# Closing units in dead activations 4 to 7, earlier opening splits, and the norm's offset added to turned rows

## The reference, cut to what matters

```python
m = hybrid_mixer(x, w_in[l], w_out[l], ...)   # projections, three kinds of attention, output projection
x = layer_norm(ALPHA * x + m, ln1_g[l], ln1_b[l])
hdn = jnp.square(jax.nn.relu(x @ w_up[l]))
x = layer_norm(ALPHA * x + hdn @ w_down[l], ln2_g[l], ln2_b[l])
# layer_norm: (x - mean) * rsqrt(var + eps) * g + b
```

## Time and profile before

| what | us |
|---|---|
| median of 3 runs | 2462.69 (2461.88 to 2463.31) |
| the profiled execution | 2461.92 |
| its span on the core | 2460.2 |
| PE busy | 2431.0 (99% of the span) |
| DVE busy | 1492.9 (61%) |
| ACT busy | 1114.3 (45%) |
| POOL busy | 85.7 (3%) |

### The profile page before, as it was taken

One profiled execution on the slowest core, in us unless ns is written; L12 is line 12 of the kernel. 1 busy time (PEld: TensorE's weight loads), 2 busy tenths in 40 slices (PEclk: granted clock), 3 DMA queues, 4 the chain that ended last, 5 costly groups with the idle time before them and its releaser, 6 DMA issues.

```text
span 2460.2 us, 30027 instructions
## 1 busy us (share of the span) xinstructions
PE 2431.0 (99%) x12624; PEld 2068.1 (84%) x12624; DVE 1492.9 (61%) x1966; ACT 1114.3 (45%) x1489; POOL 85.7 (3%) x94
## 2 busy tenths in 40 slices
PE   9999999999999999999999999999999999999997
PEld 8888888878888888888878888888788888888886
DVE  5576666676556556556665765665765555655566
ACT  4445444444345344344444444543453443443443
POOL 3000000030000000000110000000300000000001
PEclk9999999999999999999999999999999999999999
DMA  8545555655665555555555545556455555556553
GB/s 303 171 158 181 169 168 170 234 173 187 210 197 190 191 188 190 196 191 186 180 166 175 175 161 169 169 170 239 171 189 191 185 199 194 188 189 190 192 196 106
DMA packets 229590, 457.94 MB, mean 186 GB/s; under 512 B 7344, under 2 KB 12208, under 8 KB 228304
## 3 DMA queue, kind: packets, MB, share of 16 engines
q1 hardware_dynamic: 227840, 444.89, 54.5%
q0 software_dynamic: 1616, 11.14, 1.2%
HBM read 452.33 MB, written 3.67 MB: 185 GB/s over the span
## 4 chain that ended last, share of the span: by engine, by line
PE 94%; DVE 4%; ACT 1%; issue 0%; DMA 0%; SPq 0%; ACTq 0%; DVEq 0%
PE pw L469 33%; PE pw L473 16%; PE pw L488 14%; PE pw L490 14%; PE pw L489 14%; DVE w_lo L981 1%; PE pa L545 1%; DVE y L1073 1%; PE pa L621 1%; ACT y L857 1%; PE pa L542 1%; DVE act_a L1042 0%; DMA y<-in_x_dram 0%; ACT w_hi L749 0%; PE pa L629 0%
## 5 line engine op out<-in xcount | busy, mean ns | idle before, releaser
L981 DVE TENSOR_TENSOR w_lo<-raw,w_hi 128x1024 fp32r<-128x1024 f32 (+1 forms) x820 | 985.7, 1217 | 685.2 <-ACT w_hi L749 677.1
L749 ACT ACTIVATE w_hi<-raw 128x1024 fp32r<-128x1024 f32 (+1 forms) x820 | 848.1, 1046 | 1000.3 <-PE pw L490 526.2
L469 PE MATMUL pw<-act_a,w_hi 128*128 128x512 f32 x3456 | 1089.3, 396 | 0.0
L473 PEld LDWEIGHTS pw<-act_a,w_lo 128*128 128x128 f32 x3456 | 649.2, 188 | 153.2
L473 PE MATMUL pw<-act_a,w_lo 128*128 128x256 f32 x3456 | 679.2, 278 | 0.0
L469 PEld LDWEIGHTS pw<-act_a,w_hi 128*128 128x128 f32 x3456 | 528.1, 189 | 1.7
L488 PE MATMUL pw<-w_hi,act_b 128*128 128x512 f32 x1216 | 474.3, 390 | 0.1
L490 PE MATMUL pw<-w_hi,act_b 128*128 128x512 f32 x1216 | 473.2, 389 | 0.0
L489 PE MATMUL pw<-w_lo,act_b 128*128 128x512 f32 x1216 | 473.2, 389 | 0.0
L490 PEld LDWEIGHTS pw<-w_hi,act_b 128*128 128x128 f32 x1216 | 228.2, 188 | 47.8
L488 PEld LDWEIGHTS pw<-w_hi,act_b 128*128 128x128 f32 x1216 | 228.2, 188 | 47.2 <-DVE act_b L1231 0.9
(11 more groups left out here) (151 smaller groups left out, 1100.4 us busy)
## 6 DMA issues: line engine op xcount, KB each, us to landing
raw<-in_w_in_dram SPq DMA_DIRECT2D x128, 1024.0 KB, 5.0
raw<-in_w_up_dram SPq DMA_DIRECT2D x128, 1024.0 KB, 5.3
raw<-in_w_down_dram SPq DMA_DIRECT2D x128, 1024.0 KB, 5.1
raw<-in_w_out_dram SPq DMA_DIRECT2D x32, 1024.0 KB, 5.1
work<-in_ln_g_dram POOLq DMA_DIRECT2D x4, 1024.0 KB, 5.0
work<-in_ln_b_dram POOLq DMA_DIRECT2D x4, 1024.0 KB, 7.4
raw<-in_w_in_dram SPq DMA_DIRECT2D x8, 288.0 KB, 2.9
y<-in_x_dram SPq DMA_DIRECT2D x4, 512.0 KB, 11.0
```

The lines of the kernel that those rows point to most:

```text
L469: nc.tensor.matmul(pw[:, b, :], hi[:, i, cols], act_a[:, k].rearrange("p a t -> p (a t)"), start=(k == 0), stop=False)
L473: last = nc.tensor.matmul(pw[:, b, SEQ:2 * SEQ], lo[:, i, cols], act_a[:, k, 0, :], start=False, stop=(k == KT - 1))
L749: nc.scalar.activation(unit_hi(c, u), raw[:, PAIR * u:PAIR * (u + 1), 0:WIDTH[c]], ACT.Copy) \
L981: V.tensor_tensor(unit_lo(c, u), raw[:, PAIR * u:PAIR * (u + 1), 0:WIDTH[c]], unit_hi(c, u).bitcast(F32), ALU.subtract).then_inc(lo_ready, 1)
```

## The change

It has five parts.

- **Closing units.** Units 4 to 7 of a closing chunk, instead of 0 to 3, lie in the dead activations `act_a`; units 0 to 3 lie in the ring, and are split when the chunk before frees it.
- **Opening splits.** ACT's high splits of opening units 0 to 3 and DVE's low splits 0 to 2 move from `open_block` to the end of `close_block`, among `centre` and `gain`. Opening unit 4 + i waits for closing unit 2i + 1 instead of 7. In `open_block` all four groups of tile 1 are taken, instead of two here and two in the next chunk.
- **The offset.** b of the first three norms is loaded by SP as rows (`b_rows`), turned once (`turn_offsets`) and kept as 48 columns (`b_col`). The turned group no longer has b: `turn_x` waits for `gained`, and `take_x` and `take_x_lo` add a column of b as they read PSUM, in four instructions of 128 columns each instead of one of 512.
- **The residual.** POOL's additions of b to `y` leave the norm: `residual(n)` waits for the last group of tile 1 (`a_ready`), and then for each token tile adds b over all 2048 columns and scales. The last norm keeps `add_offset`. `lambda_sums` of layer 1 waits for the scaling.
- **The turned hidden rows.** PE's two `turn_hidden` move from the opening chunk's unit 5 and the next chunk's unit 1 to units 4 and 5 of the next chunk; the high and low takes of them to its units 6 and 7; `take_hidden_rows` of tile 0 from behind split 2 to behind split 1.

```diff
@@ -286,30 +291,29 @@
-    if CLOSING[c] and u < RING:
-        return act_a[:, LOAD * u:LOAD * u + PAIR].rearrange("p k a t -> p k (a t)")
+    if CLOSING[c] and u >= RING:
+        return act_a[:, LOAD * (u - RING):LOAD * (u - RING) + PAIR].rearrange("p k a t -> p k (a t)")
     if OPENING[c] and u >= RING:
 def unit_lo(c, u):
-    if CLOSING[c] and u < RING:
-        return act_a[:, LOAD * u + PAIR:LOAD * (u + 1)].rearrange("p k a t -> p k (a t)")
+    if CLOSING[c] and u >= RING:
+        return act_a[:, LOAD * (u - RING) + PAIR:LOAD * (u - RING + 1)].rearrange("p k a t -> p k (a t)")
     if OPENING[c] and u >= RING:
-    if CLOSING[c]:
-        if u < RING:
-            return (c - N_OUT if c % NC == LAST_OUT else c - N_OUT, UNITS - 1)
-        return c - 1, u
+    if CLOSING[c] and u >= RING:
+        return c - N_OUT, UNITS - 1
     if OPENING[c] and u >= RING:
-        return c - 1, UNITS - 1
+        return c - 1, PAIR * (u - RING) + 1
     if u >= RING:
         return c, u - RING
-    return c - 1, u if c > 0 and OPENING[c - 1] else u + RING
+    return c - 1, u if OPENING[c] or c > 0 and OPENING[c - 1] else u + RING
...
@@ -326,6 +330,14 @@
+    def load_offsets():
+        for layer in range(DEPTH):
+            for i, src in enumerate((ln1_b, ln2_b)):
+                n = 2 * layer + i
+                if n < 2 * DEPTH - 1:
+                    nc.sync.dma_start(b_rows[n * KT:(n + 1) * KT, :],
+                                      src[layer:layer + 1, :].rearrange("l (k p) -> (l k) p", p=P)).then_inc(b_landed, 16)
...
@@ -414,9 +427,18 @@
-        pool.wait_ge(xt_ps, x_count(e, t, LOADS - 1))
         nc.gpsimd.tensor_scalar(y[:, t, :], y[:, t, :], ALPHA, 1.0, ALU.mult, ALU.mult).then_inc(y_scaled, 1)
+    def residual(n):
+        e = n + 1
+        pool.wait_ge(ln_landed, 32 * (n + 1))
+        pool.wait_ge(a_ready, x_count(e, TT - 1, LOADS - 1))
+        for t in range(TT):
+            nc.gpsimd.tensor_tensor(y[:, t, :], y[:, t, :], ln_b, ALU.add).then_inc(offset_done, 1)
+            pool.wait_ge(offset_done, TT * n + t + 1)
+            scale_y(e, t)
+        pool.wait_ge(y_scaled, TT * (e + 1))
...
@@ -425,26 +447,21 @@
     for t in range(TT):
+        pool.wait_ge(xt_ps, x_count(0, t, LOADS - 1))
         scale_y(0, t)
         load_ln(layer, ln1_g, ln1_b)
-        pool.wait_ge(ln_landed, 64 * layer + 32)
-        for t in range(TT):
-            for j in range(LOADS):
-                add_offset(2 * layer, t, j, x_ready)
-            scale_y(2 * layer + 1, t)
-        pool.wait_ge(x_ready, norm_count(2 * layer, TT - 1, LOADS - 1))
+        residual(2 * layer)
         load_ln(layer, ln2_g, ln2_b)
-        pool.wait_ge(ln_landed, 64 * layer + 64)
-        for t in range(TT):
-            for j in range(LOADS):
-                if layer + 1 < DEPTH:
-                    add_offset(2 * layer + 1, t, j, x_ready)
-                elif t == 0 or j % 2 == 0:
-                    add_offset(2 * layer + 1, t, j, out_ready[t][j])
-            if layer + 1 < DEPTH:
-                scale_y(2 * layer + 2, t)
+        if layer + 1 < DEPTH:
+            residual(2 * layer + 1)
+    n = 2 * DEPTH - 1
+    pool.wait_ge(ln_landed, 32 * (n + 1))
+    for t in range(TT):
+        for j in range(LOADS):
+            if t == 0 or j % 2 == 0:
+                add_offset(n, t, j, out_ready[t][j])
...
@@ -509,7 +526,7 @@
         else:
-            pe.wait_ge(x_ready, norm_count(e - 1, t, j))
+            pe.wait_ge(gained, norm_count(e - 1, t, j))
             if t > 0:
...
@@ -529,6 +546,11 @@
+    def turn_offsets():
+        pe.wait_ge(b_landed, 16 * (2 * DEPTH - 1))
+        n = (2 * DEPTH - 1) * KT
+        nc.tensor.transpose(pa[:, 3, SEQ:SEQ + n], b_rows[:], ident[0:n, 0:n]).then_inc(b_turned, 1)
...
@@ -710,8 +732,8 @@
                         feature_unit(c, u)
-                        if (quarter, j, u) == (0, 1, 1):
-                            turn_hidden(layer, 1)
+                        if (quarter, j) == (0, 1) and 4 <= u < 4 + TT:
+                            turn_hidden(layer, u - 4)
                         continue
...
@@ -770,9 +792,16 @@
         act.wait_ge(xt_ps, x_count(e, t, j))
-        slot = (TT * j + t) % HC if e == 0 else j
-        nc.scalar.activation(act_a[:, HC * j:HC * (j + 1), 0, t * P:(t + 1) * P],
-                             pa[:, slot, :].rearrange("p (i t) -> p i t", i=HC), ACT.Copy).then_inc(a_hi, 1)
+        if e == 0:
+            slot = (TT * j + t) % HC
+            last = nc.scalar.activation(act_a[:, HC * j:HC * (j + 1), 0, t * P:(t + 1) * P],
+                                        pa[:, slot, :].rearrange("p (i t) -> p i t", i=HC), ACT.Copy)
+        else:
+            for i in range(HC):
+                k = HC * j + i
+                last = nc.scalar.activation(act_a[:, k, 0, t * P:(t + 1) * P], pa[:, j, i * P:(i + 1) * P], ACT.Identity,
+                                            bias=b_col[:, (e - 1) * KT + k:(e - 1) * KT + k + 1])
+        last.then_inc(a_hi, 1)
...
@@ -862,27 +891,32 @@
         for j in range(LOADS):
+            if n < 2 * DEPTH - 1 and j % 2 == 0:
+                split_hi(c + 1, j // 2)
             centre(n, 0, j)
+        if n < 2 * DEPTH - 1:
+            split_hi(c + 1, 2)
+            split_hi(c + 1, 3)
         e = n + 1
-        split_hi(c, 0)
+        if n == 0:
+            act.wait_ge(b_col_ready, 1)
         take_x(e, 0, 0)
-        split_hi(c, 1)
-        split_hi(c, 2)
+        split_hi(c, 4)
         take_x(e, 0, 1)
-        split_hi(c, 3)
+        norm_seed(n, 1)
         take_x(e, 0, 2)
-        split_hi(c, 4)
+        split_hi(c, 5)
         take_x(e, 0, 3)
-        split_hi(c, 5)
-        norm_seed(n, 1)
+        centre(n, 1, 0)
         split_hi(c, 6)
-        centre(n, 1, 0)
+        centre(n, 1, 1)
+        centre(n, 1, 2)
         split_hi(c, 7)
-        for j in range(1, LOADS):
-            centre(n, 1, j)
-        for j in range(2):
+        centre(n, 1, 3)
+        for j in range(LOADS):
             take_x(e, 1, j)
...
@@ -908,6 +940,10 @@
                     act.wait_ge(kidx_ps, layer + 1)
+                    if layer == 0:
+                        act.wait_ge(b_turned, 1)
+                        nc.scalar.activation(b_col[:], pa[:, 3, SEQ:SEQ + (2 * DEPTH - 1) * KT], ACT.Copy) \
+                            .then_inc(b_col_ready, 1)
                     nc.scalar.activation(k_idx_t[:], pa[:, 3, 0:SEQ], ACT.Copy).then_inc(kidx_sb, 1)
...
@@ -949,12 +985,8 @@
                 split_hi(c, u)
-                if j == 1 and u < 2:
-                    take_x(2 * layer + 1, 1, 2 + u)
-                if (j, u) == (1, 3):
-                    turned_hidden_hi(layer, 0)
-                if (j, u) == (1, 5):
-                    turned_hidden_hi(layer, 1)
+                if j == 1 and u >= UNITS - TT:
+                    turned_hidden_hi(layer, u - (UNITS - TT))
                 if u == AHEAD - 1 and KIND[c - 1] == "feature":
...
@@ -1038,11 +1070,19 @@
         dve.wait_ge(a_hi, x_count(e, t, j))
-        slot = (TT * j + t) % HC if e == 0 else j
-        V.tensor_tensor(act_a[:, HC * j:HC * (j + 1), 1, t * P:(t + 1) * P],
-                        pa[:, slot, :].rearrange("p (i t) -> p i t", i=HC),
-                        act_a[:, HC * j:HC * (j + 1), 0, t * P:(t + 1) * P].bitcast(F32), ALU.subtract) \
-            .then_inc(a_ready, 1)
+        if e == 0:
+            slot = (TT * j + t) % HC
+            last = V.tensor_tensor(act_a[:, HC * j:HC * (j + 1), 1, t * P:(t + 1) * P],
+                                   pa[:, slot, :].rearrange("p (i t) -> p i t", i=HC),
+                                   act_a[:, HC * j:HC * (j + 1), 0, t * P:(t + 1) * P].bitcast(F32), ALU.subtract)
+        else:
+            for i in range(HC):
+                k = HC * j + i
+                last = V.scalar_tensor_tensor(out=act_a[:, k, 1, t * P:(t + 1) * P], in0=pa[:, j, i * P:(i + 1) * P],
+                                              scalar=b_col[:, (e - 1) * KT + k:(e - 1) * KT + k + 1],
+                                              in1=act_a[:, k, 0, t * P:(t + 1) * P].bitcast(F32),
+                                              op0=ALU.add, op1=ALU.subtract)
+        last.then_inc(a_ready, 1)
...
@@ -1080,6 +1120,9 @@
         dve.wait_ge(lam_landed, 16 * (layer + 1))
+        if layer > 0:
+            dve.wait_ge(y_scaled, TT * (2 * layer + 1))
         did(V.tensor_tensor(lam_products, lam_pairs[:, :, 0, :], lam_pairs[:, :, 1, :], ALU.mult))
...
@@ -1277,29 +1320,32 @@
         for j in range(LOADS):
+            if n < 2 * DEPTH - 1 and j < 3:
+                split_lo(c + 1, j)
             gain(n, 0, j)
         e = n + 1
-        split_lo(c, 0)
+        if n == 0:
+            dve.wait_ge(b_col_ready, 1)
         take_x_lo(e, 0, 0)
-        split_lo(c, 1)
-        split_lo(c, 2)
+        split_lo(c, 3)
         take_x_lo(e, 0, 1)
         aggregate(1)
-        split_lo(c, 3)
+        split_lo(c, 4)
```

(39 more changed lines are left out.)

## The result

The changed kernel takes 2486.94 us (median of 5 runs, 2486.58 to 2489.05), the kernel before 2462.69: 24.3 us more, a ratio of 1.0102 with an interval of 1.0091 to 1.0113. The forecast was 2482, a range of 2463 to 2490, and slower with a chance of 0.77. The profiled execution took 2486.95 with a span of 2485.1, so the spans differ by 24.9.

What follows compares the result with a forecast made beforehand. PE, busy 2431.0 of 2460.2 us, was taken as the bound, with only holes and tail to win. Terms 4.2 - 6.3 - 1.6 + 18.6 + 4.1 + 0.2 = +19.2 us gave 2482 us, range 2463 to 2490.

Steps and rivals of the forecast that it cites:

- The closing chunk: Four closings: DVE's additions with statistics delay unit 4, a hole of 0.9 us, with restart 1.05; +4.2 us in all.
- S+6.35: S is the closing chunk's start; unit 4 was to be ready 6.35 us later, where PE needs it at 5.44.
- The opening chunk: Three openings: earlier splits and no POOL work there start token tile 1 sooner despite finer 128-column instructions; -6.3 us.
- The walk: Step-by-step timing of DVE's opening-chunk instructions, with PE meeting waits of 0.6, 0.5, 1.4 and 0.8 us.
- T+28.15: T is token tile 1's start in the closing chunk; the opening's tile 1 was to start 28.15 us later, against 30.24 before.
- Hidden rows: Moving the turned hidden rows to the next chunk's units 4 and 5 removes a 0.8 us wait, twice; -1.6 us.
- POOL's offset: Behind the first and third boundary, 2048-column additions hold DVE 4.6 us each, so a hidden-rows bank frees late; +18.6 us.
- The rivals that let DVE in or hid POOL's work: DVE gets in during or ahead of POOL's long instruction: some 2466 us, chance 0.16; POOL's work hidden: 2459, 0.10.
- The 144-column chunk: At the second boundary low splits take turns with POOL, delaying unit 3 by 3.1 and unit 4 by 1.0 us; +4.1.
- PE stands for 9.3 us in total in unit 0, twice: PE's wait for hidden-rows banks in the next chunk's first unit, at the first and third boundary; +18.6 us.
- the bank's own term: PE's waits for the hidden-rows banks at the first and third boundary, forecast at +18.6 us.

Runs made afterwards that it cites:

- the closing part alone: The kernel before with only the closing units changed, 4 to 7 in the dead activations and 0 to 3 in the ring: 2466.17 us, ratio 1.0017.
- The run in pieces: The changed kernel with POOL's offset additions in pieces of 512 columns at the same place, scaling still 2048 wide: 2464.73 us, ratio 1.0010.
- the late start: The changed kernel with POOL's residual work after the hidden rows are taken (norms 0, 2) or the 144-column chunk is split (norm 1): 2462.02 us.
- the rows taken one split earlier: The changed kernel with DVE taking the hidden rows of token tile 1 behind low split 2 instead of 3: 2476.36 us, ratio 1.0057.
- the filled stands: The changed kernel with products nobody reads ahead of PE's long waits behind the norms, 30 or 9 of them: 2478.01 us.

## Why the prediction was right, and where it was short

- **The closing chunk.** The step was DVE's two additions in front of low split 4. Unit 4 was to be ready at S+6.35 and PE to lose 1.05; it lost 1.02 in each of four closings, and the closing part alone, on the kernel before, cost 4.07 us for 4.2.
- **The opening chunk.** The walk put token tile 1 at T+28.15, and it came at T+27.8. All four holes are where they were placed, at group 2 (0.4), split 5 (0.5), split 6 (1.3) and tile 1's first group (0.8). The finer instructions were sized well: DVE's group of four lasts 1.13 us with its last end (forecast 1.06 back to back), ACT's 1.13 (1.1).
- **Hidden rows.** Their wait in the opening chunk went, 0.95 us a time with the restart for 0.8 without it.
- **POOL's offset.** This step gave the sign. The strict turns, POOL's waiting instruction ahead of DVE's next, the hold of 4.6 us for 2048 columns and the bank freed at T+51.6 were the forecast; measured were the same turns, holds of 4.4 to 4.6 and T+50.4. The run in pieces shows that the instruction's length is paid, the late start shows that the 17 us go with POOL's place, and the rows taken one split earlier show which wait it was. The rivals that let DVE in or hid POOL's work are out: the two splits beside an addition lasted 5.5 and 5.6 us.
- **The 144-column chunk.** The same turns; 2.8 us for 4.1. DVE's first two splits there were 0.6 us ahead of the walk, and the second hole was 0.5 for 1.0.
- **What failed is a term that the sum did not have.** "PE stands for 9.3 us in total in unit 0, twice" was priced as the stand alone. The products behind it ran at half the clock, 9.8 us over the three boundaries, more than half of the bank's own term, and the largest share of it behind the shortest stand, at norm 1. The Trainium skill, "TensorE: Matmul & The Clock Gate", section "Part 1: The HAM clock gate (the "warmup" mystery)", names an idle array as what throttles it; the filled stands agree with it, 1.00 throughout. Without this term the measured ones sum to +15.1, where the forecast has +19.2: it was 4.1 us too high (1.7 in the bank, 1.3 in the 144-column chunk, 1.1 in the openings), and that cancels part of the 9.8 that were missing. The forecast is nearer to the result than its own reasons were: 5 us off, by luck in so far as 4.1 too much stood against 9.8 too little.
- **A loose reading.** The four waits of PE that the prediction calls the largest are the four at the norms; the first turn's wait for x at the start of the kernel, 2.5 us, is larger than two of them. Nothing in the sum rests on it.

**What stays open.** How long the clock stays down behind a stand differs between runs of the same structure (6.8, 8.1, 8.2 and 9.9 us of weighted busy time behind norm 1 in four kernels with that stand), and was not looked into. What the three small loads and the one transpose cost at the start of the kernel was not tried alone, and 0.6 us is within what that point moves between profiles. The earlier opening splits were not undone by themselves.

## What to carry to other kernels

When elementwise work is moved to GpSimd "beside" VectorE, each VectorE operation with two SBUF inputs can wait for one whole GpSimd instruction, so the price is the length of that instruction, once for each such operation in front of the urgent one: look at what stands in VectorE's queue, and who waits for it. Begun after the last urgent operation the same work was free at norms 0 and 2; in pieces at the old place it still left stands of 2.5 and 1.4 us. And a stand of TensorE has a second price behind it, so a forecast that finds a stand of some microseconds adds products at half speed. That price was largest where narrow products followed, at norm 1; that their width is the reason was not shown.

## What the runs showed of the hardware that was not expected

The clock fell in or right behind stands of 1.9 us (hidden rows earlier, norms 0 and 2), 2.1 us (norm 1, after), 2.5 us (in pieces, norm 0) and 7.3 us, and did not fall with stands of 1.4 us (in pieces, norm 2) or with the three of 1.5, 1.4 and 0.9 us within 9 us (late POOL work, norm 1). Behind norm 1 in the kernel after and norm 0 with the hidden rows earlier it fell 1.0 and 1.5 us after PE had gone on. Behind norm 1, where 144-column products follow, it stayed at the lower level for 14 us with PE recorded busy for 12.85 of 13; behind the other norms, with 512-column products, for 3 to 4 us of them, and up to 5.5 in the variants. The addition of two inputs over 2048 columns holds VectorE off for 4.6 us on GpSimd, 3.6 times that over 512 (1.29). When both wait, the engine whose instruction was waiting first goes next, in strict turns.
